# A hybrid decoder layer: 208 tokens gather their v rows instead of 104, gate products in fp32r, low parts of v on DVE, rows laid out earlier

## The reference, cut to what matters

```python
s = jnp.einsum('thsk,hsnk->thsn', q, keys)        # 8 heads, 2 halves, 128 keys each
s1, i1 = lax.top_k(s[:, :, 0], 16); s2, i2 = lax.top_k(s[:, :, 1], 16)
cand_s = s1[..., :, None] + s2[..., None, :]      # 256 candidates a head
top_s, pos = lax.top_k(cand_s, 16)                # 16 experts a head, 128 a token
idx = jnp.take_along_axis(i1 * 128 + i2, pos, -1)
g = jax.nn.softmax(top_s, -1)
act = jax.nn.gelu(jnp.einsum('tkd,td->tk', u_tab[idx], xb))
out = jnp.einsum('tk,tkd->td', g * act, v_tab[idx])
```

## Time and profile before

| | |
|---|---|
| median of 3 runs | 2122.35 us (2120.17 to 2128.44) |
| the profiled execution | 2119.71 us, its span in the trace 2117.9 us |
| first product, first to last start on TensorE | 505.6 to 1339.2 us |
| second product, first to last start | 1340.7 to 2096.3 us |
| busy: TensorE, DVE, ACT, POOL | 92%, 54%, 33%, 47% of the span |
| moved by DMA | 432.15 MB, 204 GB/s over the span |

### The profile page before, as it was taken

One profiled execution on the slowest core, in us unless ns is written; L12 is line 12 of the kernel. 1 busy time (PEld: TensorE's weight loads), 2 busy tenths in 40 slices (PEclk: granted clock), 3 DMA queues, 4 the chain that ended last, 5 costly groups with the idle time before them and its releaser, 6 DMA issues.

```text
span 2117.9 us, 32667 instructions
## 1 busy us (share of the span) xinstructions
PE 1948.4 (92%) x12935; PEld 1754.4 (83%) x12935; DVE 1137.8 (54%) x2844; ACT 698.3 (33%) x1233; POOL 994.7 (47%) x796
## 2 busy tenths in 40 slices
PE   7889997989999999999999999789998898898996
PEld 2774654788999999999999999678887888788886
DVE  4949923303999947777676741334434533343342
ACT  1321114323333334444444444222322332232233
POOL 1540001242554453333333334477777777777762
PEclk8998589999999999999999999899999999999998
DMA  7533044332888877788888879866777776677641
GB/s 233 157 82 106 1 157 151 99 111 86 234 227 229 229 224 209 239 244 248 240 247 242 241 243 301 266 224 235 260 244 253 243 250 235 227 239 251 240 166 50
DMA packets 305111, 432.15 MB, mean 204 GB/s; under 512 B 23264, under 2 KB 225168, under 8 KB 302912
## 3 DMA queue, kind: packets, MB, share of 16 engines
q1 hardware_dynamic: 285456, 372.64, 56.6%
q0 software_dynamic: 19504, 57.44, 8.4%
HBM read 364.78 MB, written 132.35 MB: 235 GB/s over the span
## 4 chain that ended last, share of the span: by engine, by line
PE 71%; POOL 14%; DVE 5%; DMA 4%; issue 3%; ACT 2%; SPq 1%; DVEq 0%; ACTq 0%
PE ps L1594 35%; PE ps L1621 15%; PE ps L1423 6%; POOL gathered_act L597 5%; POOL v_rows_ring L606 5%; PE ps L1583 4%; POOL hl L589 4%; PE ps L1370 3%; DMA gbp<-gate_spill 2%; PE ps L1504 2%; PE ps L1502 1%; ACT hl L784 1%; PE ps L1546 1%; PE ps L1387 1%; PE ps L1519 1%
## 5 line engine op out<-in xcount | busy, mean ns | idle before, releaser
L589 POOL TENSOR_TENSOR hl<-raw,hl 128x512 fp32r<-128x512 f32 x512 | 684.5, 1346 | 660.7 <-ACT hl L784 659.5
L1594 PE MATMUL ps<-h,hl 128*128 128x256 f32 (+1 forms) x6144 | 831.2, 288 | 0.0
L1594 PEld LDWEIGHTS ps<-h,hl 128*128 128x128 f32 x6144 | 764.1, 189 | 0.1
L1621 PE MATMUL ps<-WH,hl 128*128 128x416 f32 x3072 | 616.3, 363 | 88.8 <-POOL hl L589 79.5
L1621 PEld LDWEIGHTS ps<-WH,hl 128*128 128x128 f32 x3072 | 596.8, 196 | 120.9 <-issue 103.0
L784 ACT ACTIVATE hl<-raw 128x512 fp32r<-128x512 f32 x512 | 322.3, 632 | 965.0 <-PE ps L1594 487.0
L1336 DVE SCALAR_TENSOR_TENSOR x_res<-ps,mods,x_res 128x416 f32<-128x416 f32 x128 | 83.2, 650 | 294.9 <-PE ps L1621 294.8
L1274 DVE TENSOR_SCALAR ohA<-ps,selT 128x128 f32<-128x128 f32 x416 | 145.5, 350 | 138.1 <-PE ps L1583 127.0
L1302 DVE TENSOR_TENSOR wf<-hring,gbp 128x416 f32<-128x416 f32 x128 | 102.5, 801 | 136.8 <-DMA gbp<-gate_spill 136.2
L1275 DVE TENSOR_SCALAR ohB<-ps,selT 128x128 f32<-128x128 f32 x416 | 167.6, 403 | 0.0
L1583 PE MATMUL ps<-ohB,ohA 128*128 128x128 f32 x832 | 159.5, 273 | 1.5 <-DVE ohB L1275 1.5
(11 more groups left out here) (276 smaller groups left out, 1468.3 us busy)
## 6 DMA issues: line engine op xcount, KB each, us to landing
raw<-in_u SPq DMA_DIRECT2D x128, 512.0 KB, 6.4
v_rows<-in_v SPq DMA_DIRECT2D x128, 512.0 KB, 5.7
raw<-in_v SPq DMA_DIRECT2D x128, 512.0 KB, 4.3
act_spill<-actr SPq DMA_DIRECT2D x128, 260.0 KB, 2.5
raw<-in_w_ada SPq DMA_DIRECT2D x64, 512.0 KB, 4.5
gate_spill<-stage SPq DMA_DIRECT2D x26, 1024.0 KB, 7.6
hring<-act_spill SPq DMA_DIRECT2D x128, 208.0 KB, 4.2
gbp<-gate_spill SPq DMA_DIRECT2D x16, 1664.0 KB, 9.1
```

Source lines behind the costliest of these rows:

```text
L589: pool.tensor_tensor(hl[:, n % 2, 1, c], raw[:, n % NRAW, c], hl[:, n % 2, 0, c].bitcast(F32), ALU.subtract).then_inc(s_wlo, 1)
L1594: last = pe.matmul(ps[:, 2 * (m % 2) + h, 0:b - a], hl[:, m % 2, w, q * P:(q + 1) * P], h2[:, r, q, a:b], start=q == 0 and (w, r) == (0, 0 ...
L1621: last = pe.matmul(ps[:, mm % 2, 0:ND], hl[:, mm % 2, w, j * P:(j + 1) * P], WHL[b % 2][:, r, j, :], start=j == 0 and (w, r) == (0, 0), st ...
```

## The change

**Split of the tokens.** `TPD` goes from 4 to 3: 312 tokens are dense (products of 312 columns in the second product), 208 gather. The 52 groups lie four in nine steps. Their sums are taken in two sets of 26 groups, in banks 6, 7 and 4, 5, each copied, transposed and added when its set ends. The rings of gathered rows and activations hold three groups instead of two.

**Gates.** The high part of each gate is rounded to fp32r and the rest kept beside it. DVE makes one-hots for four tokens with three operations, the second factor twice (times the high and times the low gate), and TensorE adds two fp32r products of 128 columns for each token, in steps 38 to 102. A store of gates holds 24 tokens instead of 16. Two token tiles are selected between the one-hots instead of one.

**Low parts of v.** From the third v tile on, DVE makes them instead of POOL, at the end of its round: two `low_half` behind `low`.

**Row copies.** 64 of the 128 are issued in the prologue, two behind each `load(n)` of tiles 56 to 87, and one in each of steps 0 to 63 of the first product; none after it.

```diff
-GBLK = 16
-TPD = NTT - 1
+GBLK = 24
+TPD = NTT - 2
-GATE0 = 50
+GATE0 = 38
-VR0 = 6
+VR0 = 4
+VG = 3
+EARLY_ROWS = 64
...
             for n in range(2, NPRE):
                 load(n)
+                i = n - (NPRE - 8 - EARLY_ROWS // 2)
+                if 0 <= i < EARLY_ROWS // 2:
+                    v_rows(2 * i)
+                    v_rows(2 * i + 1)
...
-                if m < PRE:
-                    v_rows(m)
+                if m + EARLY_ROWS < (NK if EARLY_ROWS else PRE):
+                    v_rows(m + EARLY_ROWS)
...
-            for m in range(PRE, NK):
-                v_rows(m)
...
-            for n in range(NK + 2, 2 * NK):
-                for half in range(2):
-                    low_half(n, half)
-                mm = n - NK - 2
-                if mm == 0:
-                    pool.wait_ge(s_vrow, 16 * NK)
-                    for c in range(NGT):
-                        gather_v(0, c)
-                g = group_of(mm + 2)
-                if g is not None and g + 1 < NGG:
-                    gather_acts(g + 1)
-                    for c in range(NGT):
-                        gather_v(g + 1, c)
+            pool.wait_ge(s_vrow, 16 * NK)
+            for c in range(NGT):
+                gather_v(0, c)
+            for g in range(1, NGG):
+                gather_acts(g)
+                for c in range(NGT):
+                    gather_v(g, c)
...
             def one_hots_until(count):
                 while made[0] < min(count, ND):
-                    tok = made[0]
-                    after(dve, s_tok, tok - OHR + 1)
-                    s = tok % OHR
-                    dve.tensor_scalar(ohA[:, s, :], ps[:, 7, 0:P], selT[:, 0, tok:tok + 1], None, ALU.is_equal)
-                    dve.tensor_scalar(ohB[:, s, :], ps[:, 7, 0:P], selT[:, 1, tok:tok + 1], selT[:, 2, tok:tok + 1],
-                                      ALU.is_equal, ALU.mult).then_inc(s_oh, 1)
-                    made[0] += 1
+                    t = made[0]
+                    after(dve, s_tok, t + 4 - OHR)
+                    s = t % OHR
+                    e = ohe[:, t // 4 % 2]
+                    after(dve, s_oh, t - 4)
+                    dve.tensor_tensor(e, iotas([P, 4, P]), selT[:, 1, t:t + 4].rearrange(
+                        "p (t o) -> p t o", o=1).broadcast_to([P, 4, P]), ALU.is_equal).then_inc(s_ohe, 1)
+                    dve.tensor_tensor(ohA[:, s:s + 4, :], iotas([P, 4, P]), selT[:, 0, t:t + 4].rearrange(
+                        "p (t o) -> p t o", o=1).broadcast_to([P, 4, P]), ALU.is_equal)
+                    dve.wait_ge(s_ohe, t // 4 + 1)
+                    dve.tensor_tensor(ohB[:, s:s + 4, :, :], e.rearrange(
+                        "p t (o n) -> p t o n", o=1).broadcast_to([P, 4, 2, P]), gate_pairs(t).rearrange(
+                        "p t (a o) -> p t a o", o=1).broadcast_to([P, 4, 2, P]), ALU.mult).then_inc(s_oh, 4)
+                    made[0] += 4
...
-                pe.matmul(ps[:, 4 + g % 2, i * P:(i + 1) * P], ohA[:, tok % OHR, :], ohB[:, tok % OHR, :],
-                          start=True, stop=True).then_inc(s_tok, 1)
+                for a in range(2):
+                    last = pe.matmul(ps[:, 4 + g % 2, i * P:(i + 1) * P], ohA[:, tok % OHR, :], ohB[:, tok % OHR, a, :],
+                                     start=a == 0, stop=a == 1)
+                last.then_inc(s_tok, 1)
...
                 if mm + JB < NK:
                     low(mm + JB)
+                if mm + 2 < NK:
+                    for half in range(2):
+                        low_half(NK + mm + 2, half)
```

More of the change, by code:

```diff
@@ L374, in build, with lows_ready, acc_bank @@
         SELC = 3
+        def lows_ready(eng, n, halves):
+            if n < NK + 2:
+                eng.wait_ge(s_wlo, 2 * n + halves)
+            else:
+                eng.wait_ge(s_vlo, 2 * (n - NK - 2) + halves)
         def slot_token(m, q):
             slot = (m - GATE0) * KD + q
[L380 removed]
+            slots = (GATE1 - GATE0) * KD
+            if not 0 <= slot < slots or (slot and (slot - 1) * ND // slots == slot * ND // slots):
                 return None
[L382 removed]
+            return slot * ND // slots
         def tokens_before(m):
[L386 removed]
+            slots = (GATE1 - GATE0) * KD
+            slot = min(slots, max(0, (m - GATE0) * KD))
+            return -(-slot * ND // slots)
         def group_of(mm):
[L391 to L392 removed]
+            pace = NGG // (NGA // 2)
+            g = (mm - VR0) * pace // 9
+            return g if mm >= VR0 and g < NGG and (mm == VR0 or (mm - 1 - VR0) * pace // 9 != g) else None
+        SET_END = {mm + 1: group_of(mm) // NGA for mm in range(NK)
+                   if group_of(mm) is not None and group_of(mm) % NGA == NGA - 1}
+        def acc_bank(s):
+            return 6 - 2 * s
         block = base.enter_context(nc.Block())
@@ L824, in gate_copy @@
             def gate_copy(g):
-                step, i = divmod(g, 4)
+                step, i = divmod(g, GPB)
                 if i == 0 and step >= 2:
@@ L855, in _ @@
                         act.activation(selT[:, kind, 0:ND], ps[:, 4 + kind, 0:ND], ACT.Copy).then_inc(s_gev, 1)
+                    act.wait_ge(s_gev, SELC)
+                    act.activation(gph[:], selT[:, 2, 0:ND], ACT.Copy).then_inc(s_gh, 1)
                 if m == GCH - 3:
@@ L1279, in _ @@
+                    dve.wait_ge(s_ohe, t // 4 + 1)
[3 more added lines that the diff above has]
+                    made[0] += 4
             one_hots_until(OHR)
-            select(TPD, lambda share: one_hots_until(OHR + int(share * (ND - OHR))))
+            for t in range(TPD, NTT):
+                select(t, lambda share: one_hots_until(OHR + int((t - TPD + share) / (NTT - TPD) * (ND - OHR))))
@@ L1285, in row_indices @@
             def row_indices():
-                dve.wait_ge(s_gev, SELC + NGS * 4 + 1)
-                link(dve.tensor_scalar(idf[:], iota[:, 0:NG], float(ND), None, ALU.add))
+                dve.wait_ge(s_gev, SELC + NGS * GPB + 1)
+                for t in range(TPD, NTT):
+                    last = dve.tensor_scalar(idf[:, (t - TPD) * TT:(t - TPD + 1) * TT], iota[:, 0:TT], float(t * TT), None, ALU.add)
+                link(last)
                 tt_ = selT[:, :, ND:T]
@@ L1562, in chosen_g @@
                 pe.wait_ge(s_top, 2)
+                pe.wait_ge(s_gev, SELC + GPB * NGS)
                 for kind in range(3):
-                    last = pe.transpose(ps[:, 6, kind * NG:(kind + 1) * NG], selv[0:TT, TPD, kind, :], ident[0:TT, 0:TT])
+                    for t in range(TPD, NTT):
+                        last = pe.transpose(ps[:, 4 + kind, (t - TPD) * TT:(t - TPD + 1) * TT], selv[0:TT, t, kind, :],
+                                            ident[0:TT, 0:TT])
                 last.then_inc(s_selp, 1)
```

137 lines of the change are left out of this document (84 added, 53 removed).

## The result

The changed kernel takes **2151.0 us** (median of 7 runs, 2138.8 to 2154.6), the kernel before 2124.2 beside it: 1.010 times as long, 95% interval 1.008 to 1.012. The prediction was 2040, with a range of 1965 to 2120.

What follows compares the result with a forecast made beforehand. TensorE, busy 92% of the span, was taken as the bound, idling mostly for POOL's low parts in the second product. Prologue +50, first product -27, second product -105 sum to -82: 2119.7 - 82 = 2038, told as 2040 us, range 1965 to 2120.

Steps and rivals of the forecast that it cites:

- Prologue, +50: Prologue: row copies between weight tile loads delay everything behind them by 50 us (45 to 93).
- The rival that they hide: Prologue: the 64 row copies slip in without delaying the tiles, total 1990 us; chance 8%.
- First product, -27: First product: fewer dense tokens with narrow fp32r products save 30 us, the start costs 3, sum -27 us.
- that rival: First product: each narrow fp32r product costs a whole fp32 one's 0.221 us, total 2114 us; chance 15%.
- Second product, -105: Second product: falls from 756 to 651 us, -105 (-180 to -40).
- Gate batches, 74 us: Second product: TensorE loses 5.3 us waiting on each of 14 gate batches, 74 us (42 to 112).
- it has only gathers left, 52 groups at 10.1 us are 525 us, less than TensorE's path: Second product: POOL's 80 us wait goes, as its gathers take 525 us, less than TensorE's path.
- DVE "fits, just": Second product: DVE's own work takes 2.9 us of each 3.43 us step, so it fits.
- DMA as bound: Second product: at about 304 GB/s, DMA traffic of 216 MB takes 710 us, total 2097 us; chance 12%.
- The port: Second product: POOL's gathers hold up DVE's operations on two SBUF operands, total 2227 us; chance 13%.
- slower 17%: Whole kernel: the chance given to the change making it slower, 17%.
- the 1.1 that I had named: Second product: sign of being wrong, DVE's two-operand operations exceeding 1.1 us.

Runs made afterwards that it cites:

- a1: The changed kernel with its row copies moved out of the prologue into the first product: 2108.4 us, 0.991 of the kernel before.
- a2: The changed kernel with each gate batch issued eight steps earlier: 2148.4 us, 1.008 of the kernel before.
- a4: The changed kernel gathering activations only for the first three groups, all v rows still gathered (output wrong): 2036.9 us, second product 632 us.
- b1: The changed kernel with POOL writing zeros in place of the small activation gathers after the first three groups (output wrong): 2053.8 us, second product 653 us.
- c3: The changed kernel with row copies in the first product, two groups of gathered rows, and three tiles instead of two for v's split parts: 2043.2 us.
- b4: The kernel before with only the low parts of v moved from POOL to DVE, from the third tile on: 2056.7 us, ratio 0.968.
- d4: The changed kernel, from the fourth group on without activation gathers and with v rows of one token in four (output wrong): 1984.3 us, second product 583 us.

## Why the prediction was wrong, point by point

**Prologue, +50: right.** 52 us; the window shows a share of 1.03 at 286 GB/s, and a1 takes the copies out and gets 51 back. The rival that they hide is gone.

**First product, -27: right in kind, 8 us off.** On ACT's timeline the gelus lie 5.77 us apart without tokens and 6.82 with them (34.12 us for five steps):

```profile
599.05 0.65 ACT L841 ACTIVATE actr<-ps 128x256 f32<-128x256 f32 x2
604.82 0.65 ACT L841 ACTIVATE actr<-ps 128x256 f32<-128x256 f32 x2
...
1003.23 0.65 ACT L841 ACTIVATE actr<-ps 128x256 f32<-128x256 f32 x2
...
1037.35 0.65 ACT L841 ACTIVATE actr<-ps 128x256 f32<-128x256 f32 x2
```

1.05 us for 4.8 tokens is 0.22 a token, 0.110 for each fp32r product of 128 columns, where I took 0.100. A token costs what it did in one fp32 product; only their number fell. By the Trainium skill (TensorE: Matmul & The Clock Gate, Back-to-back issue gap) it would be 0.081; the trace doesn't agree here. The two narrow products don't cost 0.442 together, so that rival is gone too. TensorE stood for 4.6 us before the first token, where I had allowed 3.

**Second product, -105: the step that failed.** I summed 651: 439 for products, 100 for row sums, 74 for gate batches, 26 for clock, 12 for sets and the first gather. The products and row sums came as sized (48 products take 7.12 us, a group 1.92 where it isn't stretched). The rest, 112 us, measured 204 (743 less 539): TensorE's gaps hold 130 of it. At the lower clock TensorE spent 106 us, 27 of them idle, so the clock cost it about 39, half of the other 79.
- *Gate batches, 74 us:* wrong here. a2 removed them and nothing changed.
- *"it has only gathers left, 52 groups at 10.1 us are 525 us, less than TensorE's path":* this is the sentence that failed. I priced a gather as 1.25 us of POOL and its bytes, and never asked what 208 small gathers do to other engines while the row gathers run. a4 and b1 put 90 us on that, 743 less 653. That my miss is 92 is partly chance, since the terms of the sum were off both ways: the 74 us for gate batches weren't there, and POOL's queue, the rows and the clock cost more than I gave them. POOL's full queue, which I called not limiting, is 21, and three quarters of the row traffic 49.
- *DVE "fits, just":* its operations were sized right, 2.9 us of 3.43. But I put two low halves in its round that wait for a step just ended, and counted their time, not what stands behind them when that wait runs long. c3 moves the wait one step back and regains 60 us.

**The rivals.** DMA as bound looked right at first (I had said 304 GB/s; the loop shows 297), and would have been believed from the profile alone; a4 moved 351 and was faster. The port gave the sign, slower (1.0% measured, where I had given slower 17%), for the wrong reason: DVE's two-operand operations took 0.48 and 0.69 us in the mean, the longest of them 0.78, short of the 1.1 that I had named, and gathers 1.0. The rule that I had cited for it (the Trainium skill, SBUF — State Buffer, Who interferes with whom) shows no price in these rows.

**What stays open.** Why TensorE's counts come late and its row sums halt. In the trace the update for step 60's first half and that for its second stand 0.13 us apart, with twelve products of 0.143 us between them, so at least the first was held back. Whether the signal or the product was held can't be told for the others: matmuls' ends are modelled. Why the low parts' move to DVE brings them (0 late tiles before, 19 in b4) wasn't taken apart. How much of the 90 us goes through the late signals isn't shown either: c3 hides 60 us of the loss and leaves 41 tiles late. Nor was it tried to gather activations without 4-byte pieces; by the table I estimate that it could bring up to 90 us with a ring of two.

## What to carry to other kernels

Price a gather by what it does to the others, not by its engine's time and bytes: 208 gathers of 4-byte pieces cost 34 us beside a quarter of the row gathers and 111 beside all of them, and little beside 12, and only leaving out each kind by itself and both together showed it. A full DMA share is not a proof that bandwidth limits: look for a run that moves more. And before putting work behind a wait on the step just ended, on an engine that works in order, give the ring one more place; it was worth 60 us here, more than any of the change's parts but the one that moved low parts to DVE.

## What was unexpected of the hardware

Small and large gathers together made TensorE's finished counts reach ACT 1 to 13 us late in 44 of 120 steps and in some runs broke up row sums that wait for nothing, at full clock too (5.8 us for 1.92 in c3; 7 of the change's 52 groups). The DMA engines moved 351 GB/s beside full compute, against 297 with small pieces among them. An fp32r product of 128 x 128 by 128 columns took 0.110 us in a stream, just half of the fp32 one's 0.221. The mean clock followed the gaps: over the whole second product it was 0.99 with 21 us of them (d4) and 0.93 with 130 (the change).
